# A hybrid attention, pooling and ConvGLU block on one NeuronCore: moving bias additions, a norm's scaling and the sums of a weight product in a hand-written order

## The reference, cut to what matters

```python
# x (1, 2048, 1024) float32, one layer
h    = rms_norm(x, norm1_g)
proj = h @ w_in                       # q 512 | k 128 | v 128 | p 512 columns
q, k = rms_norm per head (64 wide)
a    = sliding_window_sink_attention(q, k, v, sinks)   # window of two chunks of 64
m    = multiscale_pool(p, pool_w, pool_b, pool_scale)  # trailing means over 2/4/8/16, minus token, 128x128 map, bias
x    = x + concat([a, m]) @ w_out
h2   = rms_norm(x, norm2_g)
u    = h2 @ w_up;  c = causal depthwise conv(3) of u
out  = x + (silu(c_gate) * c_val) @ w_down
```

## Time and profile before

| | |
|---|---|
| median of 3 runs | 1764.26 us (1764.02 to 1765.81) |
| the profiled execution's own time | 1765.85 us |
| its span | 1764.1 us |
| TensorE busy (matmul) | 1748.3 us, 99% |
| VectorE, ScalarE, GpSimd busy | 76%, 47%, 17% |
| granted TensorE clock, mean | 0.999 |

### The profile page before, as it was taken

One profiled execution on the slowest core, in us unless ns is written; L12 is line 12 of the kernel. 1 busy time (PEld: TensorE's weight loads), 2 busy tenths in 40 slices (PEclk: granted clock), 3 DMA queues, 4 the chain that ended last, 5 costly groups with the idle time before them and its releaser, 6 DMA issues.

```text
span 1764.1 us, 23493 instructions
## 1 busy us (share of the span) xinstructions
PE 1748.3 (99%) x8454; PEld 1454.6 (82%) x8454; DVE 1340.5 (76%) x1773; ACT 822.2 (47%) x1448; POOL 302.0 (17%) x296
## 2 busy tenths in 40 slices
PE   8999999999999999999999999999999999999999
PEld 7787888888888888888888888888888888888887
DVE  4656856566789888889888878878877778865874
ACT  4565645535665444444454444444444433333321
POOL 2353312434110000000000000000004023220210
PEclk9999999999999999999999999999999999999999
DMA  8867688577747433332375232232237998976883
GB/s 325 282 226 281 237 323 297 206 286 263 252 154 259 136 95 120 132 95 72 132 279 174 84 96 72 84 91 77 79 95 242 345 354 316 306 254 222 293 287 131
DMA packets 224245, 355.30 MB, mean 201 GB/s; under 512 B 14650, under 2 KB 107010, under 8 KB 223106
## 3 DMA queue, kind: packets, MB, share of 16 engines
q1 hardware_dynamic: 204702, 301.31, 50.5%
q10 hardware_dynamic: 19427, 52.49, 7.6%
HBM read 273.00 MB, written 80.74 MB: 201 GB/s over the span
## 4 chain that ended last, share of the span: by engine, by line
PE 92%; DVE 3%; DMA 1%; ACT 1%; POOL 1%; issue 1%; SPq 0%; ACTq 0%; DVEq 0%
PE ps L1037 30%; PE ps L1039 29%; PE ps L1038 29%; DVE sums L1959 1%; PE ps L1214 1%; PE ps L1337 1%; POOL ss_q L2507 1%; PE ps L1238 1%; PE ps L1225 1%; DMA wP_d<-wp_kept 0%; DVE w_lo L1899 0%; PE ps L1109 0%; DMA raw<-in_w_in_dram 0%; DMA raw<-in_w_out_dram 0%; PE ps L1201 0%
## 5 line engine op out<-in xcount | busy, mean ns | idle before, releaser
L1037 PE MATMUL ps<-va_hi,wv 128*128 128x512 f32 x1232 | 479.4, 389 | 0.0
L1039 PE MATMUL ps<-va_hi,wv 128*128 128x512 f32 x1232 | 479.3, 389 | 0.0
L1038 PE MATMUL ps<-va_lo,wv 128*128 128x512 f32 x1232 | 479.3, 389 | 0.0
L1039 PEld LDWEIGHTS ps<-va_hi,wv 128*128 128x128 f32 x1232 | 231.3, 188 | 48.0
L1037 PEld LDWEIGHTS ps<-va_hi,wv 128*128 128x128 f32 x1232 | 231.3, 188 | 47.9
L1038 PEld LDWEIGHTS ps<-va_lo,wv 128*128 128x128 f32 x1232 | 231.3, 188 | 47.8
L1037 PE MATMUL ps<-dt_hi,ds_hi 128*128 128x512 f32 x616 | 239.6, 389 | 0.0
L1038 PE MATMUL ps<-dt_lo,ds_hi 128*128 128x512 f32 x616 | 239.6, 389 | 0.0
L1039 PE MATMUL ps<-dt_hi,ds_lo 128*128 128x512 f32 x616 | 239.6, 389 | 0.0
L2311 DVE SCALAR_TENSOR_TENSOR cb<-ub,cst,cb 128x1024 f32<-128x1024 f32 x176 | 217.8, 1279 | 8.3 <-ACT cb L1736 8.3
L1736 ACT ACTIVATE cb<-ub,cst 128x1024 f32<-128x1024 f32 x88 | 109.2, 1244 | 158.2 <-DVE ub L2360 94.5
(11 more groups left out here) (223 smaller groups left out, 2894.0 us busy)
## 6 DMA issues: line engine op xcount, KB each, us to landing
dg<-gT_d SPq DMA_DIRECT2D x264, 256.0 KB, 5.4
rw<-in_w_up_dram SPq DMA_DIRECT2D x84, 512.0 KB, 5.2
dw<-in_w_down_dram SPq DMA_DIRECT2D x132, 256.0 KB, 5.5
gT_d<-cb ACTq DMA_DIRECT2D x44, 512.0 KB, 2.6
w_hi<-wA_d SPq DMA_DIRECT2D x30, 512.0 KB, 4.2
w_lo<-wA_d SPq DMA_DIRECT2D x30, 512.0 KB, 6.2
n<-in_x_dram SPq DMA_DIRECT2D x16, 512.0 KB, 8.6
raw<-in_w_out_dram SPq DMA_DIRECT2D x16, 512.0 KB, 5.0
```

Of the source, the lines that this page charges most:

```text
L1037: pe.matmul(out_ap, l_hi, r_hi, start=first, stop=False, skip_group_check=True)
L1038: pe.matmul(out_ap, l_hi, r_lo, start=False, stop=False, skip_group_check=True)
L1039: return pe.matmul(out_ap, l_lo, r_hi, start=False, stop=last, skip_group_check=True)
```

## The change

Five edits, three in the list and two in functions of VectorE:

1. In block 1, the first group of weight differences (`to_sum` 0) takes the place that the scaling of block 2's rows had (`n1sc` 2), ahead of `q` (1, 2). Its load goes ahead of SyncE's load for `q` (1, 3), and the 2 MB load of block 0's rows moves behind it. `n1sc` (2) now stands behind `inv` (1, 0).
2. `rb` of blocks 0 and 1 goes ahead of the last `inv` entry of blocks 1 and 2.
3. For block 0, `n2sc` goes ahead of `to_lo` 3 and of `win` (2, 1), and `to_sum` 3 and `to_hi` 3 go behind `av` (1, 0), (1, 1) and `n2sq` (0). For block 1, `n2sc` goes ahead of `win` (3, 1) by the same lines.
4. In `w`, the results of the last product are added ahead of the split of a later unit's weights.
5. In `q` (2, 3) and `q` (3, 3), the second of two splits goes ahead of the scaling of tile 2.

```diff
@@ attention_order(), projection of block a @@
         units("q", a, (1,))
-        if a == 1:
-            units("r_load", a, ())
...
         units("win", a, (3,))
-        if more:
+        if a == 1:
+            units("to_sum", a, (0,))
+        elif more:
             units("n1sc", a + 1, ())
...
         units("q", a, (2,))
         if a == 1:
+            units("to_load", a, (0,))
             units("bias", a, ())
-            units("to_sum", a, (0,))
...
         if a == 1:
-            units("to_load", a, (0,))
+            units("r_load", a, ())
             units("to_hi", a, (0,))
...
             units("inv", a, (0,))
+            units("n1sc", a + 1, ())
...
+            units("rb", a - 1, ())
             units("inv", a, (1,))
         else:
...
             units("w", a - 1, (6, 1))
+            if more:
+                units("rb", a - 1, ())
             units("inv", a, (1,))
-        if more:
-            units("rb", a - 1, ())
...
+            units("av", a, (0,), (1,))
+            units("n2sq", a - 1, ())
             if a == 1:
                 units("to_sum", a, (3,))
-            units("av", a, (0,), (1,))
-            if a == 1:
                 units("to_hi", a, (3,))
-            units("n2sq", a - 1, ())
...
+            units("n2sc", a - 1, ())
+            if a == 1:
                 units("to_lo", a, (3,))
             units("win", a + 1, (1,))
-            units("n2sc", a - 1, ())
@@ VectorE, the products of halves @@
             def w(b, n, i, k):
-                if i == 6:
-                    split(n + LEAD)
                 if k == 1:
                     added(b, i, 0)
                     added(b, i, 1)
+                if i == 6:
+                    split(n + LEAD)
@@ VectorE, q @@
                     if t == 2 and a - 1 in SEVEN:
                         split(UNIT["w", a - 1, 1, 0])
+                    if t == 3 and a - 1 in SEVEN:
+                        split(UNIT["w", a - 1, 1, 1])
                     if t:
                         scaled(a, t - 1)
-                if a - 1 in SEVEN:
-                    split(UNIT["w", a - 1, 1, 1])
                 scaled(a, NT - 1)
```

## The result

| | before | after |
|---|---|---|
| median, us | 1765.14 (1764.02 to 1767.16, 6 runs) | 1775.94 (1774.83 to 1777.40, 6 runs) |
| ratio to before | 1 | 1.0061, 95% interval [1.0048, 1.0074] |
| span of the profiled execution | 1764.1 | 1773.6 |

The change costs 9.5 us of span and 10.8 us of median. The forecast was 1767.3 us, its range ended at 1771.0, and it gave "slower" 0.32.

The account below looks back on a forecast made before the run. TensorE was taken as the bound, busy 1748.3 of 1764.1 us. Terms 3.1 + 3.0 - 0.46 - 2.06 - 0.54 = +3.0 us on a median of 1764.26 gave 1767.3 us, chance 0.53; range 1759.5 to 1771.0.

Parts of the forecast that it names:

- The front: Block 1, near 166 us: earlier sums of q remove TensorE's 1.85 us wait; the two moved loads cost nothing.
- The scalings beside GpSimd: Block 1, behind the reciprocals near 194 us: GpSimd holds VectorE's row scalings, so the split behind them ends 4.7 us later.
- The additions held: GpSimd's bias additions hold VectorE's 128x8 additions ahead of `hT_lo`: TensorE 3.1 us late in block 1, 3.0 in block 2.
- Rivals A and B: In order: small VectorE additions not held, 1759.8 us, chance 0.25; only the first held, 1761.0 us, chance 0.10.
- rival C: In `inv`, the reciprocals are held by GpSimd as well: 4.8 us more in each of both blocks, 1777 us, chance 0.12.
- The wins: TensorE's waits of 0.46 and 2.06 us (block 0's second norm) and 0.54 us (residual addition near 446.80) go.
- the margin of 4 us: At block 0's `t2`: scaling ends by 234.5, TensorE arrives at 238.5, so the waits go with 4 us to spare.
- The key/value loads: Behind block 1: no wait for these loads forecast; no TensorE wait seen up to 440 us that could give time back.
- The clock: One 1.2 GHz stretch goes at `t2`, one comes behind the new waits: no net change, bounds -1.7 to +1.7 us.

Follow-up runs that it names:

- x3_rload_back: Changed kernel with the 2 MB load of block 0's rows back ahead of the loads for `q` (1, 2); 1773.49 us, ratio 1.0048.
- x11_gains_loads: x7_gains_alone with the 2 MB load of `r` and the first output-weight load at the changed kernel's places; 1765.43 us, ratio 0.9998.
- x7_gains_alone: Kernel before with earlier q sums and second norm, last-product additions before splits, `n1sc` (2) where GpSimd idles; loads and bias additions unmoved; 1763.76 us.
- x5_bias_waits: Changed kernel, same order, but GpSimd starts the bias additions only once VectorE's reciprocals are done; 1768.45 us, ratio 1.0021.
- x9_store_later: Changed kernel with the store of the last output-weight product issued on SyncE behind block 2's key/value loads; 1768.53 us, ratio 1.0018.
- x1_bias_back: Changed kernel with the bias additions of blocks 0 and 1 back behind the last `inv`; 1768.50 us, ratio 1.0017.
- x4_before_bias: Kernel before with only the move of the bias additions ahead of the last `inv`; 1769.70 us, ratio 1.0026.
- x8_scaling_idle: Changed kernel with the scaling of block 2's rows moved behind `to_lo` (1, 0), where GpSimd is idle; 1772.32 us, ratio 1.0038.
- x2_split_first: Changed kernel with the split `to_lo` (1, 3) ahead of the second norm's scaling `n2sc` again; 1773.73 us, ratio 1.0045.
- x6_filler: Kernel before with 16 identity transposes on TensorE ahead of its 2.06 us wait at `t2`; 1764.40 us, ratio 0.9993.

## Why the prediction was wrong, step by step

It forecast +3.0 us and the span grew by 9.5. By its own steps:

- **The front: wrong, 2.0 us.** "I cost both at nothing" was said of the two loads. The load of `r`, taken away from in front of one load, was set down in front of another, `raw<-wP_d`, whose landing was not looked up. TensorE passed 168 us 0.12 us late in place of 1.85 us early, and VectorE came to the reciprocals at 194 us at the old time, not 2.8 us ahead. Shown by x3_rload_back and, alone, by x11_gains_loads. That the chain of sums itself would have won its 1.85 us was right: x7_gains_alone has no wait there.
- **The scalings beside GpSimd: right.** 4.7 us forecast; the split behind them ended at 201.48 in place of 197.1, 4.4 us.
- **The additions held: right in kind.** 0.82 and 2.16 us in block 1, 1.19 and 2.16 in block 2, and GpSimd took its four in 9.32 us. From the front to the probabilities of block 1 TensorE lost 6.24 (218.04 against 211.80) - 0.12 - 1.7 of clock = 4.4 us, forecast 4.95. In block 2 the wait was 1.87 us, forecast 3.0: mis-sized by 1.1 us. Rivals A and B fall with the same rows. That the additions make the loss is shown by x5_bias_waits.
- **The reciprocal, rival C: refuted.** 0.20 us each time. The Trainium skill, "SBUF — State Buffer", section "Who interferes with whom", names copy, cast and tensor_scalar and instructions with two SBUF inputs as what contends with GpSimd. Here scaling and 128x8 addition were held, the reciprocal not, and four residual additions (one input from PSUM) took 2.47 us, their own pace, though GpSimd ran from 209.05 on: the trace agrees in all four.
- **The wins: right in size, not in time.** The waits of 0.46, 2.06 and 0.54 us went, and 0.18 us at 407.21 too. But the last square of block 0 started at 231.13 and not at 228, and the scaling ended at 237.36 and not by 234.5, since all was later than forecast by then; TensorE got to `t2` only at 241.21, so the margin of 4 us held.
- **The key/value loads: missed, 3.1 us.** Behind block 1 the prediction followed the compute engines and not SyncE's queue. That `n2sc` now stands ahead of `to_lo` (1, 3), that a store waits for this split, and that the key/value weights and the loads of `n` stand behind the store in SyncE's list, was in the order of the change and was not followed. The prediction named the wait of `n2sc` for its store (it gave the landing of 3 us) and put nothing behind it. Shown by x9_store_later.
- **The clock: mis-sized, 3.4 us.** One stretch for one was taken; three came (5.1 us against 1.7). One of them hung on the missed wait at 251. The mean clock of the six executions, 0.997 against 0.999 before, agrees, so it is not luck of the profiled one. Bounds of +-1.7 us were too narrow.

The errors are +2.0 - 0.5 - 1.1 - 0.2 + 3.1 + 3.4 = +6.7, and 3.0 + 6.7 = 9.7 against 9.5 measured. Of the change's own edits, edit 2 costs most: 6.0 us of span in the changed kernel (x1_bias_back), and alone 3.1 us of waits or 4.6 us by the medians (x4_before_bias). Moving the one store wins as much (x9_store_later). The parts don't add: x1, x3, x8 and x9 win 6.0, 3.0, 4.8 and 6.6 us of 9.5 in the profiled executions, and 7.5, 2.5, 3.8 and 7.9 of 10.8 by the medians, since each takes stretches at the low clock away or brings some, and moves TensorE earlier or later at the waits behind.

Left open: why the clock falls behind one wait of 1.87 us and not behind the next, or from 10 to 20 us in two executions and not in the others; and how the 2.8 us of the two moved loads divide between them.

## What to carry to other kernels

Where instructions are issued from one list, follow each moved one to the DMA queue: what waits for it there, and which loads stand behind that. A store whose data is late belongs behind the loads, not ahead of them. A big load that is taken from in front of one transfer lands in front of another; look up who waits for that one, since 2 MB are some 6 us of all DMA engines at the rate seen here.

Tiny VectorE instructions with two SBUF operands ought not to lie on the critical path beside a train of long GpSimd ones: the second of two 0.12 us additions took 2.16 us.

A wait of TensorE of about 2 us is to be counted with the 1.7 us of clock that may follow.

## What the runs showed of the hardware that was not expected

- The clock, in the profiled executions from 130 to 460 us. All losses were 1.7 us or twice that. Behind single waits of up to 1.77 us none was seen (x5_bias_waits, after, x11_gains_loads); but from 10 to 20 us it fell in x2_split_first and x4_before_bias, where TensorE's waits from 7 to 13 us were of 0.28 to 0.79 us. Of eight waits of 1.85 to 1.88 us, those of after (339.56), x6_filler (166.77) and x2_split_first (338.58) were followed by one, those of before (168.13), x3_rload_back, x4_before_bias, x8_scaling_idle and x9_store_later were not. Behind waits of 2.06 to 2.7 us it fell in 8 of 11 cases, not at 2.29 us (x1_bias_back, 156.30) nor in x2_split_first and x3_rload_back at 2.37 us. Waits of 3.04, 3.27 and 4.55 us for the key/value loads were followed by 3.4 us of loss, one of 3.03 us in x4_before_bias by 1.7. A window of x9_store_later behind its wait of 1.88 us in block 2:
```profile
334.00:337.50 3.50, 3.49 (x25) 2.78 (x26) 3.50 (x6) 2.81 (x5) 3.50 (x2) 1.00 0.00 0
```
  The changed kernel, behind its wait of 1.87 us at the same place, has 0.54 at 341. So a change elsewhere that shifts a wait in time can win or lose 1.7 us at it, and differences of that size between two versions may say nothing about the edit.
- One filler of 2.0 us of transposes kept the clock up at its place and still won nothing that can be told; in the profiled execution the loss reappeared at another wait.
- GpSimd was slowed little by what it held up: its two scalings took 4.20 us beside VectorE's 5.97, where they took 4.73 before beside a split, and 3.75 at 218.33 beside `hT_lo`, and the four bias additions to the rows `r` took 9.32 to 9.44 us whether VectorE waited beside them or not.
